# Eleven seven-product pairs from tile pair 5 on, and the last block of the input sums half a tile pair earlier, in the feed-forward stage of a fused two-block kernel

## The reference

```python
def conv_ffn(h, w_up, conv_w, w_down):          # w_up 1024 x 5632, w_down 2816 x 1024
    gu = causal_dwconv(h @ w_up, conv_w)        # 3 taps along the tokens
    g, u = jnp.split(gu, 2, axis=-1)            # 2816 channels each
    return (jax.nn.silu(g) * u) @ w_down

x = x + conv_ffn(rmsnorm(x, norm_ffn_gain), ffn_w_up, ffn_conv_w, ffn_w_down)
```

## Time and profile before

| | |
|---|---|
| median of 3 runs | 1209.61 us (1208.76 to 1210.14) |
| the profiled execution's own time | 1209.19 us |
| its span | 1207.4 us |
| PE busy | 1194.9 us, 99% |
| DVE, ACT, POOL busy | 754.0, 649.4, 734.6 us |
| up part, tile pairs 0 to 21 | 785.81 to 1021.54 us of the span |

### The profile page before, as it was taken

The page is one execution under the profiler, slowest core; times in us unless marked ns, Lnnn a source line. Parts: engine busy times, 40 slices in busy tenths (PEclk is TensorE's granted clock), DMA queues, the critical chain, the costliest instruction groups (busy, mean ns, idle before and its releaser), DMA issues.

```text
span 1207.4 us, 19455 instructions
## 1 busy us (share of the span) xinstructions
PE 1194.9 (99%) x7027; PEld 997.9 (83%) x7027; DVE 754.0 (62%) x1366; ACT 649.4 (54%) x1259; POOL 734.6 (61%) x566
## 2 busy tenths in 40 slices
PE   9999999999999999999999999999999999999997
PEld 7987777777888899988797777778999998898886
DVE  6655426756646777646597646436888886966224
ACT  6365535676645344455644666456666664333543
POOL 6773232353359776856384557548877776986842
PEclk9999999999999999999999999999999999999999
DMA  7332222122223333363242123343333334434332
GB/s 247 105 89 84 62 62 62 53 66 76 70 62 96 93 100 96 104 186 110 55 119 62 45 70 100 93 149 93 91 98 104 103 100 112 159 97 118 109 88 70
DMA packets 63016, 116.51 MB, mean 96 GB/s; under 512 B 6920, under 2 KB 11528, under 8 KB 62408
## 3 DMA queue, kind: packets, MB, share of 16 engines
q1 hardware_dynamic: 62776, 115.25, 33.1%
q10 hardware_dynamic: 144, 0.00, 0.0%
HBM read 110.97 MB, written 4.26 MB: 95 GB/s over the span
## 4 chain that ended last, share of the span: by engine, by line
PE 81%; DVE 11%; issue 3%; ACT 2%; POOL 1%; DMA 1%; SPq 0%; DVEq 0%; ACTq 0%; POOLq 0%
PE pb L1190 18%; PE pb L1191 18%; PE pb L1193 18%; PE pb L1252 3%; PE pb L1254 3%; PE pb L1253 3%; DVE t8s L2218 2%; PE pb L1408 2%; DVE cv L2125 2%; PE pb L1261 2%; PE pb L1384 2%; PE pb L1351 1%; PE pb L1322 1%; PE pb L1324 1%; PE pb L1323 1%
## 5 line engine op out<-in xcount | busy, mean ns | idle before, releaser
L2892 POOL TENSOR_TENSOR wlo<-raw,whi 128x512 fp32r<-128x512 f32 (+2 forms) x374 | 505.3, 1369 | 327.2 <-ACT whi L1617 323.1
L1190 PE MATMUL pb<-HH,whi 128*128 128x512 f32 x696 | 282.6, 406 | 0.0
L1617 ACT ACTIVATE whi<-raw 128x512 fp32r<-128x512 f32 (+3 forms) x373 | 221.4, 615 | 107.2 <-PE pb L1193 54.8
L1191 PE MATMUL pb<-HL,whi 128*128 128x512 f32 x696 | 275.3, 395 | 0.0
L1193 PE MATMUL pb<-HH,wlo 128*128 128x512 f32 x696 | 274.5, 394 | 0.0
L1190 PEld LDWEIGHTS pb<-HH,whi 128*128 128x128 f32 x696 | 131.1, 188 | 34.6 <-issue 4.6
L1191 PEld LDWEIGHTS pb<-HL,whi 128*128 128x128 f32 x696 | 131.0, 188 | 30.9 <-issue 2.9
L1193 PEld LDWEIGHTS pb<-HH,wlo 128*128 128x128 f32 x696 | 130.9, 188 | 30.5
L1758 ACT ACTIVATE P<-P,stat 128x256 f32<-128x256 f32 (+3 forms) x96 | 50.6, 527 | 78.5 <-DVE stat L2449 56.1
L2125 DVE SCALAR_TENSOR_TENSOR cv<-pb,vecs,cv 128x511 f32<-128x511 f32 x88 | 65.6, 745 | 2.4 <-ACT cv L2022 0.8
L2892 POOL TENSOR_TENSOR wlo<-s7a,whi 128x512 fp32r<-128x512 f32 x32 | 42.4, 1326 | 30.6 <-ACT whi L1617 30.4
(11 more groups left out here) (489 smaller groups left out, 2920.9 us busy)
## 6 DMA issues: line engine op xcount, KB each, us to landing
raw<-in_wall SPq DMA_DIRECT2D x368, 256.0 KB, 2.8
raw<-in_wall SPq DMA_DIRECT2D x8, 260.0 KB, 3.1
X<-in_xT SPq DMA_DIRECT2D x8, 256.0 KB, 5.6
X<-in_xT SPq DMA_DIRECT2D x2, 1024.0 KB, 8.4
x_kept<-X SPq DMA_DIRECT2D x2, 1024.0 KB, 6.5
X<-x_kept SPq DMA_DIRECT2D x2, 1024.0 KB, 6.1
outT<-PP SPq DMA_DIRECT2D x8, 256.0 KB, 2.6
raw<-in_wall SPq DMA_DIRECT2D x10, 192.0 KB, 2.4
```

Source lines behind the costliest of these rows:

```text
L1190: pe.do.matmul(b, hi, xh[k], start=start, stop=False, skip_group_check=tile[0] == "down")
L1191: pe.do.matmul(b, hi, xl[k], start=False, stop=False, skip_group_check=tile[0] == "down")
L1617: a.do.activation(whi[u % NS][:, 0:n], x, ACT.Copy).then_inc(*up("whi", ("whi", u)))
L2892: g.do.tensor_tensor(lo, x, hi.bitcast(F32), ALU.subtract).then_inc(*up(name, point))
```

## The change

`UPS` becomes (5, 6), (8, 9), (11, 12), (14, 15), (17, 18) and 20 alone. The sums of block 3 are made in the second half of tile pair 3, and the parts of each block one tile after its sums.

```diff
-UPS = (6, 7, 9, 10, 12, 13, 15, 16, 18, 19)
+UPS = (5, 6, 8, 9, 11, 12, 14, 15, 17, 18, 20)
 NUP = NGATE + len(UPS)
...
-        sums_of = {j + 1: j for j in range(4)}
+        sums_of = {(1, 0): 0, (2, 0): 1, (3, 0): 2, (3, 1): 3}
...
-                if j in sums_of and half == 0:
+                past = (j, 0) if half else (j - 1, 1)
+                if past in sums_of:
+                    add("t_parts", 3, sums_of[past])
+                if (j, half) in sums_of:
                     for i in range(2):
-                        take(("ts", sums_of[j], i))
-                    add("t_sums", 3, sums_of[j])
-                elif j in sums_of:
-                    add("t_parts", 3, sums_of[j])
+                        take(("ts", sums_of[j, half], i))
+                    add("t_sums", 3, sums_of[j, half])
```

## The result

The changed kernel takes 1214.63 us (1214.55 to 1214.92, 5 runs) against 1209.61 us before: ratio 1.0042, interval 1.003 to 1.0055. It is 5.0 us **slower**. The forecast was 1210.0 us with a range up to 1211.8; the time lies outside it.

The account below looks back on a forecast made before the run. TensorE, busy 99% of the span, was taken as the bound. -1.36 (matmuls) + 1.8 (block 3 wait) + 0.2 (POOL) - 0.3 (U7 wait) gave +0.3 to +0.4 us, forecast 1210.0 us, range 1208.0 to 1211.8.

Parts of the forecast that it names:

- term one: Matmuls of added pair 20: seven-product pair 9.82 us instead of plain 11.18, so -1.36 us.
- the walk of block 3: Queue walk ACT, DVE, POOL to pair 5: block 3's parts ready at 847.6, PE needs them at 845.8, 1.8 us wait.
- 1.8 + 0.2 - 0.3 = 1.7: Pairs 5 to 7: 1.8 us wait for block 3, 0.2 for POOL behind it, -0.3 from a shorter U7 wait.
- Rival (a): Pair 5: block 3's parts land before 845.8, only the -1.36 us is left, 1208.0 us; chance 0.27.
- Rival (b): Pairs 5 and 6: POOL starts block 3's parts at 848, not 845; 3.8 us lost, 2.4 net, 1212.0; chance 0.07.
- term two: Pair 20's extra weight work on ACT, DVE, POOL: costs nothing; DVE has caught up, work following pair 21 starts as now.
- the 0.2 us of bank 7: Pair 5: bank 7, written by product A22, comes free at about 844.9 against 844.7, inside the 1.8 us wait.
- Faster at 0.04: Chance that the whole kernel gains more than 0.2% (2.4 us), which needs 1207.2 us, below every case.
- 0.90 on "within 0.2%": Chance that the whole kernel's time stays within about 0.2% (2.4 us), indistinguishable from no change.

## Why the prediction was wrong, step by step

**Right: term one.** The first pair of a couple (but for pair 5, which waits) and pair 20 take 9.80 us, plain pairs 11.13 to 11.17. The added pair is worth 1.43 us in the runs.

**Right in mechanism, some tenths short: the walk of block 3.** It is the part on which most of the text went; ACT's and POOL's steps held to 0.15 us, PE's to 0.2. The timelines of ACT, POOL and PE of the changed kernel:

```profile
844.01 1.05 ACT L1650 ACTIVATE tuh<-tus 128x1024 fp32r<-128x1024 f32 x1
```

```profile
845.14 2.52 POOL L2893 TENSOR_TENSOR tul<-tus,tuh 128x512 fp32r<-128x512 f32 x2 [3.23 <-ACT tuh L1650]
847.62 1.29 POOL L2893 TENSOR_TENSOR wlo<-s7a,whi 128x512 fp32r<-128x512 f32 x1
```

```profile
847.81 0.35 PE L1253 MATMUL pb<-tuh,whi 128*128 128x256 f32 x1 [1.59 <-POOL tul L2893]
```

The rounding was forecast for 843.9, the parts for 845.0 to 847.6, and PE's 22nd matmul for 847.6, 1.8 us after its place in an undisturbed pair; it came at 847.81, 2.0 us after. Pair 5 took 12.05 us, above the 11.6 to 11.9 forecast, and pair 6 10.01, above the "about 9.9". Together they cost 2.0 to 2.1 us more than a couple does elsewhere (9.81 and 10.19), where 1.8 + 0.2 - 0.3 = 1.7 was forecast.

That pair 21 nevertheless starts only 0.26 us late is in part luck. The plain pairs behind the couples took 11.13 to 11.15 us instead of 11.19, and the later second pairs of the couples 10.11 to 10.17 instead of 10.18 to 10.20, together 0.4 us that no step of the prediction had.

Rival (a), in time, is refuted here, and the kernel with the sums from (0, 1) on shows what it would have given, 1207.3 to 1207.9 us; that is below the 1208.0 at which the prediction put it, by about as much as those 0.4 us. Rival (b), POOL's lag growing, did not come about.

**Wrong: the end of the up part.** The step that failed stands in term two: "So it has caught up, and the work that follows 21 starts as now." DVE had caught up, were read rightly, and "scaled 1 21" began 1.92 us behind an idle DVE. But "the work that follows" was taken to be DVE's chain alone. PE's own next tile was left out: it needs no result of DVE, but a bank. I had followed the banks by hand around pair 5, where I found the 0.2 us of bank 7, and did not follow them to the place where the rotation meets a list written by hand. The price of what was left out: 4.0 us of wait, 1.6 us of clock, minus 0.3 us. With the 0.26 us up to pair 21 that is 5.6 us; the two profiled spans are 5.4 us apart and the medians 5.0, and the rest was not followed. The wait by the same steps would have come out rightly, as it is one scaling and four tap instructions of DVE after the last matmul, 0.44 us of start and 3.7 us of work.

**The chances.** Faster at 0.04 was sound: this edit could win 1.36 us at most. The 0.90 on "within 0.2%" counted only what had been looked at. Rival (b), the slower one, had the right sign and the wrong place.

## What to carry to other kernels

Where a planner hands out buffers in rotation and a later stage takes them from a fixed list, any edit that adds, removes or moves a single take turns the rotation, and what the later stage meets is then a matter of luck. Follow the last user of each such buffer across the border before pricing anything else, and look at what the first instruction behind the border writes, not only at what it reads. A better cure than another exchange in the table is to let the planner choose the first down bank too; this was not tried.

Moving a step earlier in order to be in time can make others late by more: the engines' queues are in order, and what counts is the distance of everything around it, not of the step alone.

## What was not expected of the hardware

A wait of about 4 us on PE is followed by nine to ten matmuls at a granted clock of 0.50 to 0.55, another 1.6 us; filling the wait with matmuls kept the clock at 1.00. The 1.6 us of idle time in pair 5 had no such consequence. The 2.2 us of idle time in pair 5 with the sums in (2, 1) and (3, 0) had it in one trace (that pair's mean clock was 0.88) and not in the other (1.00), so the length of the idle time alone does not decide it. These are single traces, and what does decide it stays open.

In the kernel before, the plain pair behind a couple takes 11.19 us and the second of a couple 10.18 to 10.20; in the kernels with couples from 5 on they take 11.13 to 11.15 and, from the second couple on, 10.09 to 10.18. Over five couples that comes to 0.4 us or so, and the kernel with ten pairs from 5 on is 0.5 us below the one before (an interval that includes no change). Turned banks as such don't do it: with the old pairs and only block 3 moved, which turns the rotation too, the pairs take 11.19 and 10.17 to 10.20 as before. The cause was not looked for and stays open.
